# Attention in a one-core transformer kernel: values as the weights of the last product, probabilities scaled before they are turned, scores two steps ahead

## The chip, the core and the metric

The kernel runs on one core of one Trainium2 chip. The metric is the time on the device in microseconds (us), as the median of several executions. A core has TensorE (PE in the profile; its weight loads are PEld), VectorE (DVE), ScalarE (ACT), GpSimd (POOL) and SyncE (SP), which issues DMAs. Each has its own list of instructions, in a fixed order, and they wait for each other by semaphores. Matrix products go from the on-chip memory SBUF to the accumulator memory PSUM, which has eight banks of 128 partitions by 512 floats. GpSimd does not work on PSUM in this kernel.

## What is computed

The reference is a two-layer model on 1024 tokens of width 1024, in float32: a hybrid mixer and a feed-forward part, then a sparse attention mixer (16 heads of 64, two key groups) and a feed-forward part. The change lies in the attention, whose three branches are weighted with gates and summed:

```python
def attend_block(args):
    ...
    p_c = masked_softmax(s_c, (dist_c >= 0)[None, :, None, None, :])        # 63 compressed keys
    o_c = jnp.einsum('bqgjn,bngd->bqgjd', p_c, v_cmp)
    imp = jnp.einsum('bqgjn,nm->bqgm', p_c, cover)
    ...
    _, top = lax.top_k(imp, top_k)                                          # 6 blocks of 64 keys
    ...
    p_s = masked_softmax(s_s, (dist_s >= 0)[:, :, :, None], axis=(-2, -1))
    o_s = jnp.einsum('bqgjkl,bqgkld->bqgjd', p_s, v_g.astype(f32))
    ...
    p_w = masked_softmax(s_w, valid_w[None, :, None, None, :])              # window of 512
    o_w = jnp.einsum('bqgjs,bsgd->bqgjd', p_w, v_blk.astype(f32))
    o = g_blk[:, :, 0, :, :, None] * o_c + g_blk[:, :, 1, :, :, None] * o_s + g_blk[:, :, 2, :, :, None] * o_w
    return o.astype(h.dtype)
...
return o @ w_out
```

## The kernel before

The attention is a list `steps` of 144 steps. A step is (branch, first head, tile of 128 queries). Branch 2 is the compressed one: eight heads in one step, 63 keys each, 16 steps. Branch 1 is the window: two heads, one to five tiles of 128 keys, 64 steps. Branch 0 is the selected one: two heads, one to eight tiles of keys, 64 steps. Steps 0 to 79 mix compressed and window steps; mostly a compressed step is followed by two window steps of five tiles and one small one. In steps 80 to 143 the selected branch runs in couples: a query tile with many key tiles, then one with few, always nine tiles together (8 and 1, 7 and 2, 6 and 3, 5 and 4); each kind of couple comes eight times.

What one window or selected step does:
- TensorE, `scores(p)` (L1625; L1615 for the compressed branch): query by key products of two heads, 64 rows each, into PSUM banks 0 to 3.
- VectorE, `bias_step` (L1244): adds the bias, takes the minimum of the row, and writes the scores to SBUF (`SR`, four buffers, so two steps). `cmp_front` (L1161 to L1167) does this for the compressed branch, and GpSimd multiplies by the slopes (L558).
- ScalarE, `exp_step` (L792; L787): the exponential, with its sum in `STAT`.
- TensorE, `turn(p)` (L1642): turns (transposes) the probabilities, four tiles of 128x128 to a PSUM bank, in banks 4 and 5 by turns.
- ScalarE, `evacuate` (L804): copies each such group to SBUF (`PTR`).
- TensorE, `values(p)` (L1670; L1664): the turned probabilities are the weights (128x128), the values move (64 columns), the result lies with queries on partitions. It is issued inside `turn(p + 1)`, in as many parts as that step has groups, or in one piece at the end where it has one or two.
- VectorE, `out_step`: reciprocal of the sum (L1256), times the gate (L1257), and then two instructions (L1267) that scale each head's result and add it to `OACC`. For the compressed branch, `cmp_back` (L1174 to L1180) sums, takes the reciprocal, multiplies the gate and sums up the importance over the heads; `cmp_out` (L1196) scales.

The orders are written out by hand. TensorE: `scores(p+1)`, `turn(p)` with `values(p-1)` in it. VectorE: `bias_step(p+1)`, `cmp_back(p)`, `out_step(p-1)`, and at some steps `importance` and `select` (L1219 to L1224), which choose the blocks. ScalarE: `evacuate(p)`, `exp_step(p+1)`. GpSimd does the 16 slope products, and then adds the block bias of each couple (L568). Behind the last step TensorE turns all of `OACC` (L1688), ScalarE copies it to `YH` (L813), VectorE makes the low part `YL` (L1287), and the output product starts (L1312), whose weights GpSimd splits in a high and a low part (L403, L406); the first two of these splits stand ahead of the attention.

## Time and profile before

| | us |
|---|---|
| median of 3 runs | 3447.17 (3446.32 to 3450.53) |
| span of the profiled execution | 3455.9 |
| TensorE matmuls busy | 3161.6 (91%) |
| VectorE busy | 1405.7 (41%) |
| GpSimd busy | 1248.5 (36%) |
| ScalarE busy | 938.8 (27%) |
| attention, first to last step | about 1908 to 2581 of the span |

The profiled execution is 8.7 us longer than the median of the runs. A row of the page's list of groups gives line, engine, operation, output and inputs with their shapes, the count, the busy time and mean ns of one, and behind the last bar the idle time of the engine ahead of it and what ended that. A row of the timeline gives the start, the length in us (of several merged instructions: until the last one ends), the engine, line and operation. A float32 matmul has two records. PEclk is TensorE's granted clock as a share of full speed.

### The profile page before, as it was taken

The page shows a single profiled execution, that of the slowest core. Times are in us where ns is not written, and L with a number is a line of the kernel's source. Part 1 is how long each engine was busy: PE and PEld are TensorE (multiplying, and loading weights), DVE is VectorE, ACT ScalarE, POOL GpSimd, SP SyncE. Part 2 cuts the span into 40 slices and gives each one's busy share as a digit, 9 for nine tenths or more (in the row PEclk, how much of TensorE's full clock was granted, in tenths as well). Part 3 has the DMA queues.
Part 4 walks back from the last instruction along what each step waited for, and adds up shares of the span by engine and source line. Part 5 has one row for each costly group of instructions (what it writes and reads, how often), then busy time and mean ns, then how long its engine had stood idle before and what let it go on. Part 6 is the DMA issues. An engine that isn't in the chain of part 4 may idle for free. (4 is left out here: it accounts for less than half of the span.)

```text
span 3455.9 us, 41720 instructions
## 1 busy us (share of the span) xinstructions
PE 3161.6 (91%) x16629; PEld 2612.9 (76%) x16629; DVE 1405.7 (41%) x2167; ACT 938.8 (27%) x1447; POOL 1248.5 (36%) x638
## 2 busy tenths in 40 slices
PE   5967889887899999999897899999999899999998
PEld 4747887765778888888685787778878688888887
DVE  3675445353333133133301676655552332232334
ACT  3332223222133011021100454446661231010121
POOL 4325323465454444444642100000004544444442
PEclk8988999998899999999998897879999899999999
DMA  3100001110111111111114000000001111111111
GB/s 132 43 25 1 1 1 31 43 55 25 43 37 48 49 49 46 52 49 44 38 49 122 9 1 1 1 1 1 1 1 37 37 48 46 47 47 50 49 46 70
DMA packets 211543, 127.46 MB, mean 37 GB/s; under 512 B 8904, under 2 KB 208077, under 8 KB 211149
## 3 DMA queue, kind: packets, MB, share of 16 engines
q1 hardware_dynamic: 209600, 125.25, 12.3%
q8 instruction: 97, 1.59, 0.2%
q10 hardware_dynamic: 1805, 0.28, 0.0%
q14 instruction: 41, 0.34, 0.0%
HBM read 112.94 MB, written 8.39 MB: 35 GB/s over the span
## 5 line engine op out<-in xcount | busy, mean ns | idle before, releaser
L403 POOL TENSOR_TENSOR WH<-WR,ONES 128x1024 fp32r<-128x1024 f32 (+1 forms) x194 | 459.8, 2370 | 1355.1 <-PE PS L1312 1280.6
L1312 PE MATMUL PS<-YH,WH 128*128 128x512 f32 x2336 | 738.5, 398 | 63.5 <-POOL YL L428 34.9
L1312 PE MATMUL PS<-YL,WH 128*128 128x512 f32 x2336 | 726.6, 393 | 0.0
L1312 PE MATMUL PS<-YH,WL 128*128 128x512 f32 x2336 | 725.0, 392 | 0.0
L1312 PEld LDWEIGHTS PS<-YH,WH 128*128 128x128 f32 x2336 | 440.8, 190 | 178.5 <-issue 53.9
L1312 PEld LDWEIGHTS PS<-YL,WH 128*128 128x128 f32 x2336 | 444.0, 190 | 93.9
L1312 PEld LDWEIGHTS PS<-YH,WL 128*128 128x128 f32 x2336 | 442.5, 189 | 93.4
L406 POOL TENSOR_TENSOR WL<-WR,WH 128x1024 fp32r<-128x1024 f32 (+1 forms) x194 | 481.1, 2480 | 15.2
L1100 DVE SCALAR_TENSOR_TENSOR X<-PS,PTF,X 128x1023 f32<-128x1023 f32 (+1 forms) x176 | 225.6, 1282 | 573.4 <-ACT X L752 560.7
L752 ACT ACTIVATE X<-PS,PTF 128x1024 f32<-128x1024 f32 x88 | 106.2, 1207 | 840.5 <-PE PS L1312 840.3
L1670 PE MATMUL PS<-X,Z 128*128 128x64 f32 x2112 | 287.4, 287 | 0.0
L1670 PEld LDWEIGHTS PS<-X,Z 128*128 128x128 f32 x2112 | 282.2, 210 | 0.0
L804 ACT ACTIVATE Z<-PS 128x512 f32<-128x512 f32 (+2 forms) x336 | 175.8, 544 | 229.1 <-PE PS L1642 228.3
L1312 PE MATMUL PS<-MH,WH 128*128 128x512 f32 x704 | 217.3, 390 | 0.0
L1312 PE MATMUL PS<-MH,WL 128*128 128x512 f32 x704 | 216.8, 389 | 0.0
L1312 PE MATMUL PS<-ML,WH 128*128 128x512 f32 x704 | 216.7, 389 | 0.0
L1642 PE MATMUL PS<-IDENT,X 128*128 128x128 f32 (+1 forms) x1184 | 201.6, 300 | 8.1 <-ACT X L787 4.7
L1642 PEld LDWEIGHTS PS<-IDENT,X 128*128 128x128 f32 (+1 forms) x1184 | 142.0, 155 | 68.1 <-issue 56.7
L792 ACT ACTIVATE X<-X,STAT 128x640 f32<-128x640 f32 (+7 forms) x256 | 185.1, 728 | 28.6 <-DVE STAT L1244 28.6
L1625 PE MATMUL PS<-X 64*128 64x512 f32 (+3 forms) x768 | 167.0, 542 | 22.6 <-DVE STAT L1244 21.9
L1312 PEld LDWEIGHTS PS<-MH,WH 128*128 128x128 f32 x704 | 131.8, 188 | 28.9 <-DVE ML L1109 1.6
L1312 PEld LDWEIGHTS PS<-ML,WH 128*128 128x128 f32 x704 | 132.1, 188 | 27.5
(302 smaller groups left out, 3264.2 us busy)
## 6 DMA issues: line engine op xcount, KB each, us to landing
WR<-in_ffn_w_up_dram SPq DMA_DIRECT2D x88, 512.0 KB, 3.8
WR<-in_hy_w_in_dram SPq DMA_DIRECT2D x28, 512.0 KB, 3.8
WR<-in_ffn_w_down_dram SPq DMA_DIRECT2D x32, 448.0 KB, 3.6
WR<-in_ffn_w_down_dram SPq DMA_DIRECT2D x16, 512.0 KB, 3.7
WR<-in_nsa_w_in_dram SPq DMA_DIRECT2D x14, 512.0 KB, 3.7
Z<-in_x_dram SPq DMA_DIRECT2D x8, 512.0 KB, 7.5
xt_scratch<-H SPq DMA_DIRECT2D x1, 4096.0 KB, 12.1
H<-xt_scratch SPq DMA_DIRECT2D x1, 4096.0 KB, 12.3
```

Of the source, the lines that this page charges most:

```text
L403: pool.tensor_tensor(WH[:, slot, 0:k, :], WR[:, slot, 0:k, :], ONES[:, :].unsqueeze(1).broadcast_to([P, k, P]), ALU.mult).then_inc(w_hi, 1)
L406: pool.tensor_tensor(WL[:, slot, 0:k, :], WR[:, slot, 0:k, :], WH[:, slot, 0:k, :].bitcast(f32), ALU.subtract).then_inc(w_split, 1)
L752: act.activation(X[:, 16 + s, :], gemm_ps(s), ACT.Identity, scale=PTF[:, bass.ds(j + tap, 1)], bias=PTF[:, bass.ds(j + (C_FBIAS + l * 2 * ...
L792: act.activation(SR[n % 4][:, 0:w], SR[n % 4][:, 0:w], ACT.Exp, scale=-1.0, bias=STAT[:, 0, n % 8:n % 8 + 1], accum_out=STAT[:, 1, n % 8:n ...
L804: act.activation(PTR[p % 2][0:rows, i * 512:i * 512 + w], PS[0:rows, 4 + g % 2, 0:w], ACT.Copy).then_inc(pt_sb, 1)
L1100: dve.scalar_tensor_tensor(out=X[:, 16 + s, d:], in0=gemm_ps(s)[:, 0:SEQ - d], scalar=PTF[:, bass.ds(j + tap, 1)], in1=X[:, 16 + s, d:], o ...
L1312: ins = pe.matmul(PS[:, 2 * slot + a, :], w[:, slot, i, :], y[:, i, a * HALF:(a + 1) * HALF], start=(i == 0 and w is WH and y is hi), stop ...
L1625: ins = pe.matmul(gemm_ps(i)[:, a:e], X[part, h // 2, chunk(qt)], X[part, kt, first * P + a:first * P + e], start=True, stop=True)
L1642: ins = pe.transpose(PS[0:rows, 4 + g % 2, (k - 4 * i) * P:(k - 4 * i + 1) * P], src, IDENT[:, :])
L1670: ins = pe.matmul(PS[:, 6 + p % 2, i * DH:i * DH + DH], PTR[p % 2][:, k * P:(k + 1) * P], X[:, (VS, VW)[b], (first + t) * P + g * DH:(firs ...
```

## The change

- `values` swaps its operands: the values (64 columns) are the weights and the turned probabilities move (128 columns). Head i of the two writes partitions 64i to 64i+63 of the PSUM bank, so the result has head dimensions on partitions and queries along the free axis. The loop runs over key tiles outside and heads inside. `turn` lays the two heads' tiles alternately.
- Scaling by reciprocal and gate moves ahead of the turn: `norm_step` on VectorE takes the reciprocal only, and GpSimd's new `scale_step` multiplies the probabilities of each head in place with reciprocal and gate (for the compressed branch one product with the scale that `cmp_back` made, which waits for all of `cmp_back`). `turn(p)` waits for `scaled` in place of `p_ready`.
- `out_step` is one addition of 128x128 (or a copy) from PSUM; `cmp_out` is a copy.
- TensorE's order is `scores(p+2)`, `turn(p)`; VectorE's `bias_step(p+2)`, `norm_step(p+1)`, `out_step(p-2)`; ScalarE's `exp_step(p+1)`, `evacuate(p)`. `SR` has six buffers (three steps); the two new ones lie where `WL` lies.
- GpSimd adds the block bias of a couple three steps ahead of it. The first two splits for the output product move behind the last turn, since `WL` is taken until then.
- Behind the last step the turning of `OACC` is gone; ScalarE and VectorE read `OACC` itself.

TensorE, the turn of a five-tile window step with the values of a five-tile step ahead of it; before:

```order
2683 L1642 MATMUL PS<-IDENT,X 128x128 [waits att_p_ready,att_pt_sb]
2684 L1642 MATMUL PS<-IDENT,X 128x128 x3
2685 L1670 MATMUL PS<-X,Z 128x64 [waits att_pt_sb]
2686 L1670 MATMUL PS<-X,Z 128x64 x2
2687 L1642 MATMUL PS<-IDENT,X 128x128 [waits att_pt_sb]
2688 L1642 MATMUL PS<-IDENT,X 128x128 [waits att_p_ready]
2689 L1642 MATMUL PS<-IDENT,X 128x128 x2
2690 L1670 MATMUL PS<-X,Z 128x64 x3
2691 L1642 MATMUL PS<-IDENT,X 128x128 [waits att_pt_sb]
2692 L1642 MATMUL PS<-IDENT,X 128x128
2693 L1670 MATMUL PS<-X,Z 128x64 x4
```

The same place in the changed kernel (L1671 turns, L1699 multiplies by the values):

```order
2683 L1671 MATMUL PS<-IDENT,SRX 128x128 [waits att_scaled,att_pt_sb]
2684 L1671 MATMUL PS<-IDENT,SRX 128x128 [waits att_scaled]
2685 L1671 MATMUL PS<-IDENT,SRX 128x128 x2
2686 L1699 MATMUL PS<-Z,X 64x128 [waits att_pt_sb]
2687 L1699 MATMUL PS<-Z,X 64x128
2688 L1671 MATMUL PS<-IDENT,SRX 128x128 [waits att_pt_sb]
2689 L1671 MATMUL PS<-IDENT,SRX 128x128 x3
2690 L1699 MATMUL PS<-Z,X 64x128 x4
2691 L1671 MATMUL PS<-IDENT,SRX 128x128 [waits att_pt_sb]
2692 L1671 MATMUL PS<-IDENT,SRX 128x128
2693 L1699 MATMUL PS<-Z,X 64x128 x4
```

As many matmuls as before; each of the values now writes 64 partitions and moves 128 columns, and both waits for the probabilities stand at the front.

GpSimd around a compressed step of the changed kernel (L560 multiplies the slopes, L568 scales a compressed step, L576 a window step; before, only the slope products stood here):

```order
395 L560 TENSOR_TENSOR SRX<-SRX,SLOPE 128x504 [waits nsa_c_sub]
396 L576 TENSOR_SCALAR X<-X,STAT,SM 128x128 [waits att_r_ready]
397 L576 TENSOR_SCALAR X<-X,STAT,SM 128x128
398 L568 TENSOR_TENSOR SRX<-SRX,CST 128x504 [waits nsa_imp_c]
399 L576 TENSOR_SCALAR X<-X,STAT,SM 128x640 [waits att_r_ready]
400 L576 TENSOR_SCALAR X<-X,STAT,SM 128x640
401 L576 TENSOR_SCALAR X<-X,STAT,SM 128x640 [waits att_r_ready]
402 L576 TENSOR_SCALAR X<-X,STAT,SM 128x640
```

The scaling of the compressed step waits for `imp_c`, the last instruction of `cmp_back`, and the two larger steps are scaled behind it.

The core of the diff:

```diff
@@ turn
-                        j, t = divmod(k, tiles)
-                        if t == 0:
-                            pe.wait_ge(p_ready, 2 * p + j + 1)
+                        if k < 2:
+                            pe.wait_ge(scaled, 2 * p + (2 if b == 2 else k + 1))
@@ values
-                    for k in mine:
-                        i, t = divmod(k, tiles)
-                        ins = pe.matmul(PS[:, 6 + p % 2, i * DH:i * DH + DH], PTR[p % 2][:, k * P:(k + 1) * P],
-                                        X[:, (VS, VW)[b], (first + t) * P + g * DH:(first + t) * P + g * DH + DH],
-                                        start=(t == 0), stop=(t == tiles - 1))
+                    for t in mine:
+                        for i in range(2):
+                            ins = pe.matmul(PS[head_part(i), 6 + p % 2, 0:P],
+                                            X[:, (VS, VW)[b], (first + t) * P + g * DH:(first + t) * P + g * DH + DH],
+                                            PTR[p % 2][:, (2 * t + i) * P:(2 * t + i + 1) * P], start=(t == 0), stop=(t == tiles - 1))
@@ gpsimd
+            def scale_step(p):
+
+                b, h, qt = steps[p]
+                if b == 2:
+                    pool.wait_ge(imp_c, cmp_no[p] + 1)
+                    pool.tensor_tensor(scores_of(p), scores_of(p), CST[:, cmp_no[p] % 2, 2, :].unsqueeze(2).broadcast_to([P, JH, NC]),
+                                       ALU.mult).then_inc(scaled, 2)
+                    return
+                w = keys_of(qt, b)[1] * P
+                pool.wait_ge(r_ready, p + 1 - cmp_no[p + 1])
+                for i in range(2):
+                    n = 2 * p + i
+                    gate = (1 + b) * H16 + h + i
+                    pool.tensor_scalar(SR[n % 6][:, 0:w], SR[n % 6][:, 0:w], STAT[:, 2, n % 8:n % 8 + 1], GATE[:, qt, gate:gate + 1],
+                                       ALU.mult, ALU.mult).then_inc(scaled, 1)
...
+            slope_step(0)
+            for p in range(len(steps)):
+                if p + 1 < len(steps):
+                    slope_step(p + 1)
+                c, before = divmod(p + 3 - SELECTED, PER_COUPLE)
+                if before == 0 and 0 <= c < len(couples):
+                    couple_bias(c)
+                scale_step(p)
+            pool.wait_ge(tr_done, pair_groups[len(steps)])
+            splits(U_NOUT, 2)
@@ vector
+            def norm_step(p):
...
+                dve.reciprocal(STAT[:, 2, at:at + 2], STAT[:, 1, at:at + 2]).then_inc(r_ready, 1)
...
             for p in range(len(steps)):
+                if p + 2 < len(steps):
+                    bias_step(p + 2)
                 if p + 1 < len(steps):
-                    bias_step(p + 1)
-                if steps[p][0] == 2:
-                    cmp_back(p)
-                if p >= 1:
-                    out_step(p - 1)
+                    norm_step(p + 1)
+                if p >= 2:
+                    out_step(p - 2)
@@ scalar
             for p in range(len(steps)):
-                evacuate(p)
                 if p + 1 < len(steps):
                     exp_step(p + 1)
+                evacuate(p)
+            act.wait_ge(o_used, len(steps))
             for m in range(MT):
-                act.wait_ge(ot_ready, m + 1)
-                act.activation(YH[:, m, :], gemm_ps(m % 2), ACT.Copy).then_inc(ot_hi, 1)
+                act.activation(YH[:, m, :], OACC[:, m, :], ACT.Copy).then_inc(ot_hi, 1)
@@ tensor
             scores(0)
+            scores(1)
             for p in range(len(steps)):
-                if p + 1 < len(steps):
-                    scores(p + 1)
+                if p + 2 < len(steps):
+                    scores(p + 2)
                 turn(p)
             values(len(steps) - 1, 0, 1)
-            pe.wait_ge(o_used, 2 * len(steps))
-            for m in range(MT):
-...
```

## Rows read from the trace of the kernel before

**Rows 1.** Groups by line and shape, 1908 to 2597 us: the values matmul.

```profile
L1670 PE MATMUL PS<-X,Z 128*128 128x64 f32 x2112 | 287.4, 287 | 0.0
```

**Rows 2.** Windows: stretch, its length, busy us of each engine (count), granted clock.

```profile
1908.00:2230.00 322.00, 300.36 (x2111) 251.66 (x2112) 221.26 (x610) 157.50 (x365) 22.21 (x25) 0.84 0.00 1
2230.00:2305.00 75.00, 67.70 (x360) 51.42 (x357) 44.65 (x143) 33.60 (x86) 4.47 (x4) 0.73 0.00 1
2305.00:2581.00 276.00, 273.50 (x2123) 224.30 (x2121) 140.92 (x518) 182.02 (x416) 13.55 (x12) 1.00 0.01 1
```

**Rows 3.** Timeline of one couple of eight and one tiles, selected branch.

```profile
2309.42 1.99 PE L1625 MATMUL PS<-X 64*128 64x512 f32 x8
...
2311.61 3.68 PE L1670 MATMUL PS<-X,Z 128*128 128x64 f32 x32
...
2312.80 1.15 ACT L792 ACTIVATE X<-X,STAT 128x1024 f32<-128x1024 f32 x1 [0.55 <-DVE STAT L1244]
...
2315.22 0.49 PE L1625 MATMUL PS<-X 64*128 64x128 f32 x4
...
2315.65 1.09 PE L1642 MATMUL PS<-IDENT,X 128*128 128x128 f32 x8
...
2317.74 1.09 ACT L804 ACTIVATE Z<-PS 128x512 f32<-128x512 f32 x2 [0.26 <-PE PS L1642]
...
2318.30 1.99 PE L1625 MATMUL PS<-X 64*128 64x512 f32 x8
```

**Rows 4.** Timeline of TensorE in the earlier mixer: matmuls with 64-column weights.

```profile
725.21 0.38 PE L1510 MATMUL PS<-IDENT,X 128*128 128x128 f32 x2
725.78 0.45 PE L1525 MATMUL PS<-H 128*64 128x128 f32 x4 [0.19 <-issue]
...
727.33 0.44 PE L1526 MATMUL PS<-H 128*64 128x128 f32 x4
727.70 1.13 PE L1531 MATMUL PS<-H 128*128 128x256 f32 x4
```

**Rows 5.** Groups by line and shape, GpSimd over the whole span.

```profile
L403 POOL TENSOR_TENSOR WH<-WR,ONES 128x1024 fp32r<-128x1024 f32 x162 | 391.7, 2418 | 1184.7 <-PE PS L1312 1110.1 <-DMA WR<-in_nsa_w_out_dram 55.0 <-DMA WR<-in_hy_w_in_dram 19.6
...
L568 POOL TENSOR_TENSOR Z<-Z,SM 128x1024 f32<-128x1024 f32 x2 | 3.8, 1900 | 0.0
...
L552 POOL TENSOR_SCALAR_AFFINE_SELECT Z<-Z 128x1024 f32<-128x1024 f32 x1 | 1.1, 1087 | 0.1
```

**Rows 6.** Line L558: ns min/median/max, first and last start of its 16 instructions.

```profile
L558 POOL TENSOR_TENSOR X<-X,SLOPE x16: 1027/1028/1031, 1934.3 to 2208.6; 128x504 f32<-128x504 f32 x16
```

**Rows 7.** Timeline around compressed steps.

```profile
2149.82 0.81 DVE L1244 CUSTOM_DVE_ANT_0 X<-PS,X 128x640 f32<-128x640 f32 x1
...
2151.31 0.67 DVE L1174 TENSOR_REDUCE CST<-X 128x8 f32<-128x504 f32 x1
...
2153.38 1.06 DVE L1180 TENSOR_REDUCE Z<-Z 128x63 f32<-128x504 f32 x1
...
2161.84 0.68 DVE L1161 TENSOR_TENSOR X<-PS,Z 128x504 f32<-128x504 f32 x1 [0.57 <-issue]
...
2164.24 1.03 POOL L558 TENSOR_TENSOR X<-X,SLOPE 128x504 f32<-128x504 f32 x1 [14.86 <-DVE X L1167]
2164.27 1.01 DVE L1257 TENSOR_TENSOR STAT<-STAT,SM 128x2 f32<-128x2 f32 x1
```

**Rows 8.** Timeline of the end of the attention.

```profile
2580.70 0.47 DVE L1267 SCALAR_TENSOR_TENSOR Z<-PS,STAT,Z 128x64 f32<-128x64 f32 x2 [1.05 <-PE PS L1670]
...
2593.81 2.36 DVE L1287 TENSOR_TENSOR YL<-PS,YH 128x1024 fp32r<-128x1024 f32 x2 [1.11 <-ACT YH L813]
2596.22 0.50 PEld L1312 LDWEIGHTS PS<-YH,WH 128*128 128x128 f32 x2 [2.61 <-DVE YL L1287]
2596.22 1.22 PE L1312 MATMUL PS<-YH,WH 128*128 128x512 f32 x2 [2.38 <-DVE YL L1287]
```

**Rows 9.** Windows of TensorE alone: length, busy us (count), granted clock.

```profile
2244.00:2246.00 2.00, 0.70 (x7) 1.00 0.00 0
2246.00:2248.00 2.00, 0.95 (x4) 0.95 0.00 0
2248.00:2250.00 2.00, 2.00 (x10) 0.50 0.00 0
```

101 lines of the change are left out of this document (49 added, 52 removed).

## Prediction, made before the changed kernel was run

> **What bounds the kernel now.** I read the shares of busy time first: TensorE is busy for 91% of the span. The change touches only the attention, 1908 to 2596 us, so I then read windows over it [rows 2]. In the selected branch (2305 to 2581) TensorE is busy for 273.5 of 276 us at full clock: it is the bound, 8.6 us per couple for 32 couples. In the compressed and window steps (1908 to 2230) it is busy for 300 of 322 us, but at a granted clock of 0.84, and VectorE is busy for 221 us; here waits on VectorE and a clock that falls behind them cost as much as TensorE's work. A cycle of one compressed and three window steps takes 15.9 us where it runs undisturbed (GpSimd's slope product comes 14.86 + 1.03 us after the one ahead of it [rows 7]) and 18.3 us on average ((2208.6 - 1934.3) / 15 [rows 6]). Last I read the timeline of one couple [rows 3]: scores, the values of the step ahead and the turn follow each other with hardly a gap.
>
> **Values as weights.** Before, 32 records (8 tiles, two heads) go from 2311.61 to 2315.22 [rows 3], 0.11 us each, 0.44 us per tile for both heads. The new form stands in the trace already: the earlier mixer multiplies with 64-column weights and writes the two halves of the partitions alternately. There seven groups of four records go by between 725.78 and 727.33 [rows 4], 0.055 us each, although each moves 128 columns, twice as many as L1670. The two halves run side by side. So a tile costs 0.22 us, half. The selected branch has 288 of the 528 tiles (2112 records / 4 [rows 1]), and the saving there is 288 x 0.22 = 63 us.
>
> **The switch between forms.** The new form is entered from a turn and left to a turn or to scores. In the trace the first 64-column matmul starts 0.46 us after the last turn's start (725.78 against 725.21 + 0.11), where 0.11 is the pace: 0.35 lost. On the way out 0.20 goes by (727.70 against 727.33 + 3 x 0.055), 0.1 lost [rows 4]. The 0.35 may hold some of the five semaphore waits in front of that matmul, so a switch into it costs between 0.1 (as the way out) and 0.35, and a piece of values 0.2 to 0.45 in all. I take 0.3, between the ends, since two waits stand there now. By the code, values come in 106 pieces in the selected branch, 3.3 per couple: +32 us. This speaks against the change where `turn` cuts values into parts of one tile. The Trainium skill, TensorEngine Tiling (Array Packing), section Tiling Modes, says that a change of tiling mode drains TensorE; the trace agrees, since the next weight load waits for the matmul ahead. The same page, Performance Considerations, recommends just this swap for 64 columns, at up to twice the speed; by that alone, with no drain, the selected branch would save 63 us less the wait of the ring below.
>
> **A chain of waits in the selected branch.** ScalarE takes `exp_step(p+1)` only after `evacuate(p-1)`. For a couple of 8 and 1 tiles the ring is: turn of the wide step to its last copy, 3.2 us (2315.65 to 2317.74 + 1.09); two exponentials, 2 x 1.15 + 0.1 = 2.4 [rows 3]; reciprocal and semaphores, 0.3; two scalings on GpSimd; 0.1 to the next wide turn. GpSimd's new instruction has one tensor input and is not in the trace. The nearest rows at 1024 elements are 1.09 us for a select in place with one input, 1.90 for a product of two tensors, and 2.42 where it also writes fp32r [rows 5]. I take 1.05, nearest in form to the first. The ring is then 6.0 + 2.1 = 8.1 us. TensorE's own work in this couple is 8.9 - 9 x 0.22 + 2 x 0.3 = 7.5, so these eight couples wait 0.6 us each, +5. For narrower ones every term of the ring shrinks, and TensorE stays the bound. The Trainium skill, GPSIMD Engine Reference, section 3.1, gives 1.03 cycles per element at 1.2 GHz for one input, an estimate of 0.88 us for 1024; with it the ring would be 7.8 us. No row shows this instruction itself.
>
> Selected branch together: -63 + 32 + 5 = -26 us.
>
> **The compressed steps.** Before, TensorE turned the probabilities right after the exponential, and `cmp_back` ran beside it. Now the turn waits for `cmp_back` and GpSimd's product, and VectorE reaches `cmp_back(q)` only behind `bias_step(q+1)`. From the end of `scores(q+1)`: bias of five tiles 1.5 us (2149.82 to 2151.31), `cmp_back` 3.1 (2151.31 to 2153.38 + 1.06), product 1.03, as L558 [rows 7], semaphores 0.3, together 5.9. TensorE has in that time a small turn with the values of a five-tile step (0.3 + 1.1 + 0.3) and scores of five tiles (about 5/8 of the 1.9 us between 2309.42 and the next turn [rows 3], and an overhead, 1.4), 3.1 us. It stands still for 2.8 us per cycle. Against that its work shrinks: 11 tiles x 0.22 = 2.4, compressed values 16 records x 0.055 = 0.9, and about 8 pieces x 0.3 = 2.4 come on top (125 pieces in these 16 cycles). 15.9 - 0.9 - 0.6 (an idle time that goes) + 2.8 = 17.2 us. So the undisturbed cycle gets 1.2 longer, 15 x 1.2 = +18 us. The clock costs 18.3 - 15.9 = 2.4 us per cycle now; it fell to 0.5 here after 4 us in which TensorE was busy for 1.65 [rows 9]; standing still becomes more frequent, but less work is left to run slowly. I leave it at 2.4.
>
> VectorE's instructions with two SBUF inputs wait while GpSimd works: L1257 takes 1.01 us beside L558 [rows 7]. GpSimd will work about a third of the time, and some of `cmp_back` and `select` can be hit; I have no more than this row for it, up to 1 us per cycle, 0 to +15, and take 0, since GpSimd has by the order little to do in these moments.
>
> **The other steps.** Steps 64 to 79 (2230 to 2305) have 54 tiles, -12, and 16 pieces, +5: -7 us. At step 77 GpSimd waits for the last `select` and adds the first couple's bias (about 2.3 us, 1.90 for the wide half [rows 5]) ahead of the scaling that the turn waits for: bias, select (six instructions, five of them over 512 elements at the 0.7 us of L1161 [rows 7], 3.6), 2.3 and two scalings make 9 us of standing still where TensorE had some 2 before: +7. Together 0.
>
> **The end.** From the last addition to the first output product 15.5 us go by (2580.70 to 2596.22 [rows 8]). The turns go; what is left is one copy (about the 1.15 of an exponential of that size [rows 3]) and eight `YL` of 1.2 (2.36 for two), 11 us. But `YL` now has two SBUF inputs, and GpSimd's four split instructions of some 2.4 [rows 5] run beside it; they hold VectorE up by 0 to 6 us. I take 4.5: 0 in all, -4 to +2. The splits themselves stay hidden behind `YL`; TensorE waits for VectorE before and after.
>
> Sum: -26 + 18 + 0 + 0 = -8 us, made on the profiled execution of 3455.9 us; the median lies 8.7 lower and I take the difference from it: 3439 us.
>
> **Rivals.**
> 1. *The compressed steps don't add.* For it: TensorE runs at 0.84 of its clock there [rows 2], and if it is up for more of the time, 300 busy us at 0.84 have up to 48 us to give. Against it: the 2.8 us of standing still. With 0 for the cycles, and pieces at 0.2 (-11): 3447 - 37 = 3410.
> 2. *The clock decides, slower.* Each cycle's 2.8 us is about as long as the idle time ahead of the fall to half [rows 9]. If every one does, some 5 us of work run slowly and cost 2 more per cycle: 3439 + 30 = 3469. It decides from about 0.5 us per cycle on.
> 3. *GpSimd is slow.* At 1.90 us for 1024 the ring is 9.8, 8.9, 8.1 and 7.6 us for the four kinds of couple, 8.6 on average, and the saving of 26 is gone. In the window steps two scalings of 640 (2 x 0.5 more) lie behind the compressed one: +15. 3439 + 26 + 15 = 3480.
> 4. *The halves don't run side by side here* (two heads' operands from one bank and buffer): values cost as before and the pieces come on top: 63 back in the selected branch, 12 in steps 64 to 79 and some 25 in the cycles, 3539. Rows 4 speak against it; 3 in 100.
>
> **Chances.** Forecast 0.40 (its own range 3425 to 3452), rival 1 0.27, rival 2 0.18, rival 3 0.12, rival 4 0.03. A measurement of this kernel can tell about 0.2%, 7 us. Faster: rival 1 and nearly 0.6 of the forecast, 0.50. Same: 0.16. Slower: 0.34. The range 3405 to 3476 leaves out rival 4, most of rival 3 and the far ends of the other two.
>
> **What would show it.** Values records at a pace of 0.055 us, with 0.1 to 0.35 us lost on the way into each piece; couples of 8 and 1 at 8.1 us that wait for GpSimd, the others near 7.7 with TensorE without gaps; TENSOR_SCALAR of 1024 near 1.05 us; compressed steps at which TensorE waits some 2.8 us for GpSimd, and `cmp_back` ahead of it. I am wrong if the turns wait in most couples, if the granted clock of the selected branch falls below 1.00, or if the cycles keep 18 us.

## The result, and the profile of the changed kernel

The changed kernel takes 3449.45 us (median of 20 runs, 3438.31 to 3452.08), the kernel before 3438.30 us in the 20 runs beside it (3428.19 to 3450.53). The ratio is 1.0029, 95% interval 1.0017 to 1.0040: **the change makes the kernel slower by 0.3%, some 10 us**. The forecast was 3439 us and faster. The time lies within the range of 3405 to 3476; the direction is the wrong one. The three runs of the kernel before from which the prediction started (3447.17) were from the upper part of its spread; these 20 runs gather near 3429, 3438 and 3448, and what sets which of them one gets stayed open. Of the kernels further down, one execution each of fill12, oldvalues and onepiece took 5.5 to 7.8 ms; the ratios leave it out, the medians hold it and are 0.3 to 1.4 us higher for it.

The first view is that of the windows: stretch, its length, busy time (count) of TensorE, its weight loads, VectorE, ScalarE and GpSimd, granted clock, DMA share and GB/s. They answer to [rows 2].

```profile
1908.00:2230.00 322.00, 267.13 (x1858) 179.79 (x1859) 176.93 (x467) 137.52 (x320) 102.45 (x123) 0.73 0.00 1
2230.00:2305.00 75.00, 62.34 (x530) 38.64 (x529) 47.51 (x143) 46.90 (x118) 30.63 (x38) 0.99 0.00 1
2305.00:2317.00 12.00, 3.19 (x18) 2.60 (x20) 5.11 (x12) 1.55 (x3) 5.04 (x6) 0.58 0.00 0
2317.00:2571.00 254.00, 245.60 (x2172) 158.44 (x2170) 112.61 (x388) 180.69 (x424) 122.42 (x145) 0.99 0.01 1
```

Up to 2230 TensorE is busy for 267 instead of 300 us and has got less far, 1858 records instead of 2111: its granted clock is 0.73 on average where it was 0.84. Behind 2305 it stands nearly still for 9 us, and the selected branch behind it is short. GpSimd, at 22 us of 322 before, now has 102.

The cycles are counted as in [rows 6], by the first and the last slope product of the 16 compressed steps, in the timeline of GpSimd:

```profile
1932.19 1.03 POOL L560 TENSOR_TENSOR X<-X,SLOPE 128x504 f32<-128x504 f32 x1 [3.01 <-DVE X L1197]
...
2239.17 1.03 POOL L560 TENSOR_TENSOR X<-X,SLOPE 128x504 f32<-128x504 f32 x1 [3.79 <-DVE X L1197]
```

307.0 us for 15 cycles, 20.5 each; [rows 6] gave 18.3. A second profile of the kernel before (below) gives 18.5. So the cycles lose 30 us, and that is the loss; the two stages behind them gain. By landmarks (last slope product; the first bias of the selected branch on GpSimd; the end of the last values; the first output product):

| us | before, second profile | change | change minus before |
|---|---|---|---|
| 15 cycles | 277.2 | 307.0 | +29.8 |
| last slope product to first bias | 80.0 | 71.3 | -8.7 |
| first bias to last values | 283.6 | 261.0 | -22.6 |
| last values to first output product | 15.6 | 16.2 | +0.6 |

From the first output product to the end of the program it is 859.8 us in the change and 856.7 in this profile of before (859.7 in its first one), so the two spans, 3447.4 and 3445.0, differ by 2.4 us.

One bias on GpSimd serves four couples of the same kind, eight steps. Such a group of four is called a set here; its time is the distance between its bias and the next on GpSimd. The recorded expectations say "couple" for it where they give 28 to 36 us.

The waits that the prediction worked out for a compressed step are in the trace nearly to the number. Here is one compressed step, all engines:

```profile
2151.86 0.82 DVE L1270 CUSTOM_DVE_ANT_0 X<-PS,X 128x640 f32<-128x640 f32 x1
...
2153.35 0.67 DVE L1204 TENSOR_REDUCE CST<-X 128x8 f32<-128x504 f32 x1
...
2155.42 1.05 DVE L1210 TENSOR_REDUCE Z<-Z 128x63 f32<-128x504 f32 x1
...
2156.63 1.03 POOL L568 TENSOR_TENSOR X<-X,CST 128x504 f32<-128x504 f32 x1 [6.93 <-DVE Z L1210]
...
2157.80 1.94 PE L1671 MATMUL PS<-IDENT,X 128*63 128x128 f32 x8 [2.96 <-POOL X L568]
```

From the bias of the five-tile step (2151.86) over `cmp_back` (2153.35 to 2155.42 + 1.05) and GpSimd's product L568 to the turn that waits for it (2157.80) it takes 5.9 us, as worked out, and TensorE stands still for 2.96 us; 2.8 was forecast. What comes behind it is this (windows again):

```profile
2150.00:2160.00 10.00, 6.40 (x50) 4.40 (x50) 8.14 (x21) 2.93 (x7) 2.69 (x3) 0.84 0.01 2
2160.00:2170.00 10.00, 10.00 (x58) 6.73 (x54) 2.30 (x9) 4.78 (x13) 1.80 (x3) 0.50 0.01 2
```

In the 10 us in which this pause lies TensorE is busy for 6.4, and in the next 10 its granted clock is 0.50, the lower of its two levels. Two microseconds at a time, TensorE alone, around the pause of another cycle:

```profile
2020.00:2022.00 2.00, 1.64 (x16) 1.00 0.00 0
2022.00:2024.00 2.00, 0.00 (x0) 0.93 0.00 0
2024.00:2026.00 2.00, 1.40 (x7) 0.50 0.00 0
```

The clock falls within the pause and stays at 0.50 up to 2040. Nine of the 16 compressed turns have a pause of 2.95 or 2.96 us and another four one of 2.26 to 3.46, and of the 28 windows of 10 us from 1950 to 2230 only 4 are at 0.98 or more; 10 are in the second profile of before.

The values and their switches (TensorE, the turn of six tiles with which the third set begins, and behind it the scores of three tiles):

```profile
2391.06 1.09 PE L1671 MATMUL PS<-IDENT,X 128*128 128x128 f32 x8
2392.09 0.44 PE L1699 MATMUL PS<-Z,X 128*64 128x128 f32 x4
2392.47 0.66 PE L1671 MATMUL PS<-IDENT,X 128*128 128x128 f32 x4
2393.05 0.44 PE L1699 MATMUL PS<-Z,X 128*64 128x128 f32 x4
2393.42 0.92 PE L1655 MATMUL PS<-X 64*128 64x384 f32 x4
```

A turn of four transposes starts at 2392.47, and the values behind it at 2393.05: 0.58 us for 4 x 0.11, so 0.14 on the way in. The four values records take until 2393.42, 0.37 for 4 x 0.055, so 0.15 on the way out. A piece costs 0.29 us (0.3 was taken), and the pace of 0.055 is that of [rows 4], where [rows 3] had 0.11.

A couple of 8 and 1 tiles, where the wide turn was to wait for GpSimd (it answers to [rows 3]):

```profile
2456.90 1.14 ACT L823 ACTIVATE X<-X,STAT 128x1024 f32<-128x1024 f32 x1
...
2458.16 0.17 DVE L1281 RECIPROCAL STAT<-STAT 128x2 f32<-128x2 f32 x1 [1.50 <-ACT X L823]
...
2458.43 2.37 POOL L576 TENSOR_SCALAR X<-X,STAT,SM 128x1024 f32<-128x1024 f32 x2 [3.09 <-DVE STAT L1281]
...
2460.15 0.33 PE L1671 MATMUL PS<-IDENT,X 128*128 128x128 f32 x1
...
2460.85 0.98 PE L1671 MATMUL PS<-IDENT,X 128*128 128x128 f32 x7 [0.38 <-POOL X L576]
...
2462.15 1.15 PE L1671 MATMUL PS<-IDENT,X 128*128 128x128 f32 x8 [0.31 <-ACT Z L835]
```

Second exponential 2456.90, reciprocal 2458.16, two scalings of 1024 columns in 2.37 us from 2458.43 on, the wide turn's first transpose when the scores ahead of it are done (2460.15), and then 0.38 us of waiting for the second scaling and 0.31 for ScalarE's copies. The ring is there, with small pauses.

GpSimd's new instruction by width (groups, 2317 to 2572 us; mean ns of one behind the comma):

```profile
L576 POOL TENSOR_SCALAR X<-X,STAT,SM 128x1024 f32<-128x1024 f32 x10 | 11.9, 1195 | 12.2 <-DVE STAT L1281 12.2
...
L576 POOL TENSOR_SCALAR X<-X,STAT,SM 128x128 f32<-128x128 f32 x10 | 4.4, 448 | 9.4 <-DVE STAT L1281 9.4
```

1.20 us for 1024 columns, 0.45 for 128: some 0.34 us for the instruction and 0.83 ns per column. The Trainium skill, GPSIMD Engine Reference, section 3.1, has 1.03 cycles per element, an estimate of 0.86 ns per column: the slope agrees with the trace, and what the estimate of 0.88 us in the prediction left out is the 0.34.

Step 77, where the selected branch begins, and the end of the attention (which answers to [rows 8]):

```profile
2310.19 0.18 DVE L1251 TENSOR_SCALAR SM<-Z 128x32 f32<-128x32 f32 x1
2310.45 2.25 POOL L588 TENSOR_TENSOR Z<-Z,SM 128x128 f32<-128x128 f32 x2 [8.40 <-DVE SM L1251]
2312.69 1.52 POOL L576 TENSOR_SCALAR SRX<-SRX,STAT,SM 128x512 f32<-128x512 f32 x2
...
2313.60 0.45 PE L1671 MATMUL PS<-IDENT,SRX 128*128 128x128 f32 x1 [8.65 <-POOL SRX L576]
```
```profile
2571.49 0.29 DVE L1295 TENSOR_TENSOR Z<-Z,PS 128x128 f32<-128x128 f32 x1 [0.58 <-PE PS L1699]
2571.81 7.68 ACT L844 ACTIVATE YH<-Z 128x1024 fp32r<-128x1024 f32 x8 [1.74 <-DVE Z L1295]
...
2572.90 14.65 DVE L1317 TENSOR_TENSOR YL<-Z,YH 128x1024 fp32r<-128x1024 f32 x8 [1.12 <-ACT YH L844]
2574.16 3.35 POOL L406 TENSOR_TENSOR WH<-WR,ONES 128x1024 fp32r<-128x1024 f32 x1
...
2587.61 1.22 PE L1342 MATMUL PS<-YH,WH 128*128 128x512 f32 x2 [16.16 <-DVE YL L1317]
```

TensorE stands still for 8.65 us behind the last select (to 2310.37), the first bias (2.25) and the first scaling. At the end the eight `YL` take 14.65 us, 1.83 each where [rows 8] had 1.18. The first three run beside GpSimd's splits and take 2.40, 3.37 and 3.36 us, the other five 1.21, and a split takes 3.35 us where [rows 5] had 2.42.

### The profile page after: what moved, and what is told of

Read it like the earlier page. It is cut to its first block and busy times, and to the rows that moved or that the text cites. A ratio compares the mean times of both kernels' runs of the same rounds, so it can differ in the third digit from the quotient of the medians.

```text
span 3447.4 us, 41440 instructions
## 1 busy us (share of the span) xinstructions
PE 3092.4 (90%) x16565; PEld 2460.8 (71%) x16565; DVE 1347.5 (39%) x1910; ACT 933.5 (27%) x1447; POOL 1469.3 (43%) x910
## 5 line engine op out<-in xcount | busy, mean ns | idle before, releaser
L576 POOL TENSOR_SCALAR X<-X,STAT,SM 128x640 f32<-128x640 f32 (+7 forms) x170 | 133.9, 797 | 157.2 <-DVE STAT L1281 157.2
L1671 PE MATMUL PS<-IDENT,X 128*128 128x128 f32 (+1 forms) x784 | 150.3, 323 | 41.6 <-POOL X L568 27.6
L1699 PE MATMUL PS<-Z,X 128*64 128x128 f32 x2112 | 175.7, 301 | 0.0
L1655 PE MATMUL PS<-X 64*128 64x512 f32 (+3 forms) x768 | 158.2, 519 | 16.7 <-DVE STAT L1270 15.7
L1671 PEld LDWEIGHTS PS<-IDENT,X 128*128 128x128 f32 (+1 forms) x784 | 97.7, 159 | 98.6 <-issue 68.2
L1342 PEld LDWEIGHTS PS<-MH,WL 128*128 128x128 f32 x704 | 132.2, 188 | 27.5
```

The source lines that it names most:

```text
L576: pool.tensor_scalar(SR[n % 6][:, 0:w], SR[n % 6][:, 0:w], STAT[:, 2, n % 8:n % 8 + 1], GATE[:, qt, gate:gate + 1], ALU.mult, ALU.mult).th ...
L1342: ins = pe.matmul(PS[:, 2 * slot + a, :], w[:, slot, i, :], y[:, i, a * HALF:(a + 1) * HALF], start=(i == 0 and w is WH and y is hi), stop ...
L1655: ins = pe.matmul(gemm_ps(i)[:, a:e], X[part, h // 2, chunk(qt)], X[part, kt, first * P + a:first * P + e], start=True, stop=True)
L1671: ins = pe.transpose(PS[0:rows, 4 + g % 2, (k - 4 * i) * P:(k - 4 * i + 1) * P], src, IDENT[:, :])
L1699: ins = pe.matmul(PS[head_part(i), 6 + p % 2, 0:P], X[:, (VS, VW)[b], (first + t) * P + g * DH:(first + t) * P + g * DH + DH], PTR[p % 2][ ...
```

## The experiments

All ratios are against the kernel before, run on the same chip beside the kernel (its medians were 3439.6 in the first four runs, 3443.1 in the second four and 3442.4 in the last two), with 95% intervals; the change stands at 1.0029. Where kernels of different groups are compared below by their medians, the 3.5 us between these medians of before are in the difference.

### The kernel before, once more

No edit.

> The kernel before, unchanged, for a second profile: the one shown ran in 3455.9 us, above the median of 3438 over 20 runs, so differences between its trace and that of the change are not those between the medians. Theory A (the clock varies from run to run in the attention's first part): a run of about 3430 to 3440 us with the same work and waits, but a higher granted clock than 0.84 between 1908 and 2230 us or than 0.73 between 2230 and 2305 us. Theory B (the difference lies elsewhere): the same clock there, and the 10 to 20 us somewhere else.

3447.5 us (one execution), span 3445.0. Theory A's time was not met: this run is no fast one either. It shows that two executions differ where the clock does: 80.0 instead of 89.6 us from the last slope product to the first bias, while the cycles add up to nearly the same (277.2 and 274.3). Its row over the cycles and the longest pause in it:

```profile
1950.00:2230.00 280.00, 265.70 (x1842) 222.79 (x1842) 194.51 (x536) 137.90 (x320) 14.41 (x14) 0.83 0.00 1
```
```profile
2110.86 2.50 PE L1625 MATMUL PS<-X 64*128 64x512 f32 x8 [3.59 <-DVE STAT L1244]
```

Behind a `select` the scores wait 3.59 us for VectorE, and from there to 2160 the 10-us windows show 0.50 to 0.69. So the kernel before loses to the clock as well, in fewer places: [rows 9] was one of them.

### Keeping TensorE busy in the pauses: the change (fill12) and the kernel before (before_fill)

```diff
 turn, behind the wait for the PSUM bank that it writes (fill12)
+                    for _ in range(12 if b == 2 and i == 0 else 0):
+                        pe.matmul(PS[:, 4 + g % 2, 0:P], IDENT[:, :], IDENT[:, :], start=True, stop=True)
```

> The change, with 12 products of the identity with itself (128 columns, fp32, about 0.22 us each at full clock, 2.6 us together) on TensorE ahead of each of the 16 compressed turns, in the PSUM bank that the turn writes next. They compute nothing that is used. In the change's trace TensorE stands still for 2.96 us ahead of nearly every one of these turns and the granted clock then falls to 0.50 for some microseconds. Theory A (the fall of the clock is the price, the waiting alone nearly nothing more than 2.96 us a cycle): the clock stays near 1.00 between 1950 and 2230 us, the cycles take 16.7 to 17.5 us instead of 20.5 and the kernel is 30 to 55 us faster than the change, 3395 to 3420 us. Theory B (the chain of VectorE and GpSimd sets the cycle, whatever the clock): 12 more products change nothing or cost up to 16 x 1 us, 3445 to 3465 us.

3402.9 us, ratio 0.9898 (0.9870 to 0.9927). Theory A holds, to its numbers: 46 us gained over the change by adding 192 products that nobody reads.

```diff
 the kernel before, ahead of the scores that wait for VectorE behind a select (before_fill)
+            late = {first_select[g] + 3 * k + 1 + 3 for g in range(NG) for k in range(TT // 2)}
...
+                if q in late:
+                    if g >= 2:
+                        pe.wait_ge(pt_sb, g - 1)
+                    for _ in range(8):
+                        pe.matmul(PS[:, 4 + g % 2, 0:P], IDENT[:, :], IDENT[:, :], start=True, stop=True)
```

> The kernel before, with 8 products of the identity with itself (1.8 us at full clock) on TensorE ahead of the 16 scores that wait for VectorE behind a select, where TensorE stands still for 1.9 to 3.6 us in the trace and the granted clock falls to 0.50 behind most of them. Nothing uses them. Theory A (the clock makes the kernel before slow here too, and makes its runs spread from 3428 to 3457 us): the clock stays near 1.00, cycles of compressed and window steps go from 18.4 to about 16.5 us on average, 15 to 35 us are gained and the spread shrinks; then against this kernel, not against the one before, must the change be held where the clock is kept up. Theory B (the clock falls for another reason than these pauses): 0 to 10 us slower.

3421.2 us, ratio 0.9937 (0.9921 to 0.9954): 22 us, within theory A's 15 to 35, and its 6 runs lie within 11 us (3414 to 3425) where the 23 of the kernel before spread over 22. The rows over 1950 to 2230, first of fill12, then of before_fill:

```profile
1950.00:2230.00 280.00, 263.16 (x2324) 187.64 (x2321) 185.04 (x499) 149.15 (x356) 107.02 (x128) 0.96 0.01 1
```
```profile
1950.00:2230.00 280.00, 268.13 (x2034) 224.66 (x2033) 207.17 (x579) 147.41 (x345) 14.42 (x14) 0.92 0.00 1
```

0.96 and 0.92, where the change had:

```profile
1950.00:2230.00 280.00, 235.50 (x1598) 158.06 (x1597) 153.37 (x401) 118.63 (x273) 85.61 (x101) 0.72 0.00 1
```

The length of each of the 15 cycles, by the starts of the slope products:

```
before (2nd)  4.3 16.3 17.9 17.6 16.4 17.8 16.3 16.4 23.5 25.6 29.6 21.0 20.8 17.6 16.3   277.2
before_fill   4.3 16.3 17.8 17.6 16.4 17.8 16.3 18.0 22.4 20.1 22.8 15.9 19.7 19.4 16.3   261.0
change        4.1 16.2 16.3 21.5 24.2 24.0 24.0 21.7 20.9 16.9 24.9 24.0 23.5 24.1 20.7   307.0
fill12        4.1 17.7 18.0 16.8 16.8 16.9 16.8 17.0 20.4 17.2 24.5 19.8 16.8 16.8 16.8   256.7
sig           4.1 14.6 15.3 16.8 16.8 16.8 16.8 16.8 20.4 19.6 25.5 19.8 19.4 18.9 16.8   258.5
```

This is the case in five lines. With its pause filled and its clock full, a cycle of the change takes 16.8 us, half a microsecond more than the 16.3 of before. With the pauses open it takes 24 us, again and again: the pause of 2.96 us brings the clock down, at half clock the work takes longer, and the clock comes back some 4 us before the next pause. The kernel before loses most at the selects (cycles 9 to 13). Filled, the two are nearly even over the cycles (256.7 and 261.0), and the kernels stand at 3402.9 and 3421.2: **with the pauses filled in both, the change is 18 us faster by the medians** and 13 by the two ratios, whose intervals leave 2 to 25 (the runs themselves don't overlap: 3400 to 3404 and 3414 to 3425). Between the first bias and the last values, where the clock is full in both but for fill12's first microseconds, it gains 20.1 us (260.9 against 281.0). The comparison isn't quite even elsewhere: before_fill fills the pauses at the selects and fill12 those of the compressed turns, and each keeps some stretches at half clock.

The fillers have a price too. In the second and third cycle the change's pauses ahead of compressed turns are 2.48 and 1.64 us or none, and the fill of 2.9 us (4.3 at half clock) makes these cycles 17.7 and 18.0 us long, where the change has 16.2 and 16.3 and sig (next) 14.6 and 15.3.

### A shorter pause (sig)

```diff
-                link(dve.tensor_tensor(CPN, cs, rs.unsqueeze(2).broadcast_to([P, JH, NC]), ALU.mult))
+                dve.tensor_tensor(CPN, cs, rs.unsqueeze(2).broadcast_to([P, JH, NC]), ALU.mult).then_inc(cpn_ready, 1)
+                dve.wait_ge(cpn_ready, cmp_no[p] + 1)
...
-                    pool.wait_ge(imp_c, cmp_no[p] + 1)
+                    pool.wait_ge(cpn_ready, cmp_no[p] + 1)
```

> The change, with GpSimd's scaling of a compressed step released one VectorE instruction earlier: after the product that writes the copy for the importance, not after the reduction behind it (1.06 us). Theory A (the chain bias, the back half of the compressed step, scaling is what TensorE waits for): its standing still ahead of compressed turns falls from 2.96 to about 1.9 us, 16 us in all, and if the shorter pause no longer lets the clock fall, up to 45 us: 3400 to 3435 us. Theory B (something else, such as ScalarE's copies or buffers, is right behind): under 5 us.

3403.1 us, ratio 0.9898 (0.9873 to 0.9924), by releasing GpSimd's product in each compressed step one VectorE instruction earlier. Theory A's time is met, but its first part, 16 us for the shorter wait itself, hardly shows. The pause did get shorter:

```profile
2007.15 1.06 PE L1672 MATMUL PS<-IDENT,X 128*63 128x128 f32 x8 [1.60 <-POOL X L568]
```

1.60 us instead of 2.96, at a granted clock of 1.00 in all 10-us windows from 1960 to 2080. But its undisturbed cycles are 16.8 us, like those of fill12, which keeps the long chain: of the 1.06 us that came off the compressed turn nothing is left in the cycle, because the turns behind it wait 0.38 and 0.46 us for the scalings of the next step. So in these cycles the shorter chain by itself gains nothing; nearly all of the 46 us is the clock.

### The swap alone (oldvalues, oldvalues_fill)

```diff
-                            ins = pe.matmul(PS[head_part(i), 6 + p % 2, 0:P], X[:, (VS, VW)[b], ...],
-                                            PTR[p % 2][:, (2 * t + i) * P:(2 * t + i + 1) * P], ...)
+                        ins = pe.matmul(PS[:, 6 + p % 2, i * DH:i * DH + DH], PTR[p % 2][:, (2 * t + i) * P:(2 * t + i + 1) * P],
+                                        X[:, (VS, VW)[b], ...], ...)
```

> The change, with the operands of the values products in the old places: probabilities as weights, 64 columns of values moved (its output is laid out wrongly, the work and the order are the change's). It prices the swap alone. Theory A (values 0.44 against 0.22 us per tile, some 0.1 to 0.3 us lost per piece): the selected branch takes 30 to 45 us longer than in the change. In the compressed steps TensorE has some 3 us more work a cycle in front of the same chain; the total is 3480 to 3500 us where the clock there stays as in the change, and 3455 to 3475 us where the added work keeps the clock up. Theory B (the swap buys nothing, the gain of the selected branch came from the order two steps ahead): within 10 us of the change.

3538.7 us, ratio 1.0303 (1.0268 to 1.0338), above both of theory A's ranges. Its runs spread from 3521 to 3556, and the profiled one is the fastest of them. There the selected part takes 298.0 us, 37 more than in the change, as expected; the cycles take 22.7 us each at a granted clock of 0.68, which was not. TensorE has more work there and a lower clock still.

> The run with the values' operands in their old places (3539 us; its output is laid out wrongly), with 12 products of the identity ahead of each compressed turn. It parts the swap's price from the clock's. Theory A (of its 89 us over the change, 37 in the selected branch are the swap and the rest is a clock that falls even more often): the clock stays up, the cycles take 18 to 19.5 us instead of 22.7, 3470 to 3490 us. Theory B (the cycle of 22.7 us is work and waits, not clock): 3530 us or more.

3475.2 us, ratio 1.0102 (1.0086 to 1.0117), within theory A's 3470 to 3490: cycles of 19.1 us, selected part 298.1. So with the compressed turns' pauses filled the swap is worth 72 us by the medians (3475.2 against 3402.9) and 66 by the spans of the two profiles; 37 of these are in the selected part and 30 in the cycles. And the other half of the change, scaling ahead of the turn and scores two steps ahead, costs 54 us by the medians (3475.2 against before_fill's 3421.2) and 45 by the spans: 25 in the cycles, 6 in steps 64 to 79, 17 in the selected part with step 77, less 1 at the end and 2.5 ahead of the cycles. Some of that is still the clock, since this kernel's pauses at the selects aren't filled and before_fill's are.

### GpSimd's place in the selected branch (narrow)

```diff
-                w = keys_of(qt, b)[1] * P
+                w = P if b == 0 else keys_of(qt, b)[1] * P
                 pool.wait_ge(r_ready, p + 1 - cmp_no[p + 1])
```

> The change, with GpSimd's scaling in the selected branch cut to the first 128 columns of each row (the other columns stay unscaled, so the output is wrong), about 0.45 us an instruction instead of up to 1.20. It prices GpSimd's place in the selected branch. Theory A (the ring of copies, exponentials, scaling and the next wide turn sets the couples of 8 and 1 tiles, TensorE the others): the two couples whose periods are 35 and 33.8 us in the change (8 and 1) get 3 to 6 us shorter each, the couples at 29.1 to 30.5 us by under 0.5 us; 6 to 12 us in all. Theory B (GpSimd is hidden everywhere): under 2 us. Theory C (GpSimd's scaling is late in every couple): 15 us or more.

3443.6 us, ratio 1.0002 (0.9989 to 1.0016), 6 us less from the first bias to the last values (255.0 against 261.0). The fifth set (8 and 1 tiles), in the change and here:

```profile
2435.04 2.26 POOL L588 TENSOR_TENSOR Z<-Z,SM 128x128 f32<-128x128 f32 x2
...
2468.82 2.26 POOL L588 TENSOR_TENSOR Z<-Z,SM 128x256 f32<-128x256 f32 x2
```
```profile
2432.01 2.26 POOL L588 TENSOR_TENSOR Z<-Z,SM 128x128 f32<-128x128 f32 x2
...
2463.91 2.26 POOL L588 TENSOR_TENSOR Z<-Z,SM 128x256 f32<-128x256 f32 x2
```

33.8 us against 31.9, so 0.5 us for each of the four couples; the other kinds get 0.5 us shorter a set or not at all (30.5 to 30.0, 29.1 to 28.6, 29.5 to 29.7). It is theory A in kind, and its total of 6 to 12 is met at the low end; but it had 3 to 6 us for each set of 8 and 1, and 2.1 and 1.9 were measured. The ring binds in the couples of 8 and 1, and it is worth 4 us.

### The first bias behind step 77's scaling (latebias)

```diff
-                if before == 0 and 0 <= c < len(couples):
+                if before == 0 and 0 < c < len(couples):
                     couple_bias(c)
                 scale_step(p)
+                if before == 0 and c == 0:
+                    couple_bias(c)
```

> The change, with the first couple's bias on GpSimd behind the scaling of step 77 instead of ahead of it (the other couples' places stay). In the change's trace TensorE stands still for 8.65 us at the turn of step 77, behind the last select, this bias (2.25 us) and the scaling, and the granted clock is 0.60 and 0.84 in the 20 us behind it. Theory A (the order on GpSimd is the cause): the turns of steps 77 and 78 go ahead during the select, the pause of 8.65 us is cut or moved to step 79, 3 to 6 us shorter, and with the clock 5 to 10 us are gained over the change in this stage. Theory B (the select itself and the order on VectorE hold the branch's start, whoever goes first on GpSimd): the pause only moves, under 3 us.

3439.8 us, ratio 0.9989 (0.9976 to 1.0001). From the first bias to the last values it takes 253.6 instead of 261.0 us: 7.4 us gained in this place, theory A. Four of its 12 runs are near 3430 and eight near 3440, and the profiled one is of the four; its cycles took 297 us and not 307. The pause is cut from 8.65 us:

```profile
2303.61 0.30 PE L1673 MATMUL PS<-IDENT,X 128*128 128x128 f32 x1 [4.80 <-POOL X L576]
```

### All of it together (combined, onepiece)

```diff
 combined: sig, latebias, 7 products ahead of each compressed turn, 6 ahead of the scores behind a select, and
+            for _ in range(60):
+                pe.matmul(PS[:, 4, 0:P], IDENT[:, :], IDENT[:, :], start=True, stop=True)
 behind the last values
```

> The change with four things: the scaling of compressed steps released behind the product (as in the run that did this alone), the first couple's bias behind step 77's scaling, and products of the identity with itself in TensorE's pauses: 7 ahead of each compressed turn, 6 ahead of the scores that wait behind a select, 60 (13 us) behind the last values, where TensorE stands still for 16.2 us and then runs at half clock for some 6 us. Theory A (the clock is what is lost, and the pauses are free to be filled): 3403 us less about 5 for the end, less 5 to 10 for the selects, less 5 to 10 for step 77: 3380 to 3390 us, granted clock at 0.95 or more in every 10 us of the attention. Theory B (the earlier release alone has got what there is): 3398 to 3405 us.

3393.9 us, ratio 0.9859 (0.9842 to 0.9875): between the theories, 9 us better than sig or fill12 alone. 5.6 us are gained in the selected part (255.3 against fill12's 260.9) and 2 in the stage ahead of it. The cycles are not better (261.5 us): theory A wanted a clock of 0.95 or more in every 10 us, and there are stretches at 0.63 to 0.68. The end:

```profile
2521.39 13.66 PE L1729 MATMUL PS<-IDENT 128*128 128x128 f32 x120
2537.67 0.74 PE L1345 MATMUL PS<-YH,WH 128*128 128x512 f32 x2 [2.62 <-DVE YL L1320]
```

The wait at the end is as long as before (16.2 us, the 60 products fill 13.7 of it), and the ten microseconds behind it now have a clock of 1.00 where the change has 0.69. That is worth little: from the first output product to the end it takes 858.5 us here, 859.5 in fill12 and 858.0 in sig.

```diff
-                    if p >= 1 and groups <= 2:
-                        if i == groups - 1:
-                            values(p - 1, 0, 1)
-                    elif p >= 1:
-                        values(p - 1, i, groups)
+                    if p >= 1 and i == min(1, groups - 1):
+                        values(p - 1, 0, 1)
```

> The run with four things together (3394 us), with the values of a step in one piece behind the second group of the next turn, instead of a piece behind each of its three or four groups. In the selected branch that takes away 40 of 106 pieces (1, 2 and 2 for each pair of steps of 7 and 2, 6 and 3, 5 and 4 tiles; none for 8 and 1). Theory A (each piece costs some 0.3 us of TensorE, 0.15 on the way in and 0.15 on the way out, as the change's trace has it, and TensorE is the bound there): 12 us less, 3382 us; the couples at 30.5, 29.1 and 29.5 us get 1.2, 2.4 and 2.4 us shorter, those of 8 and 1 stay. Theory B (the pieces cover ScalarE's copies, which the third and fourth group wait for; in one piece that cover is lost): 0 to 5 us slower.

**3374.8 us, ratio 0.9806 (0.9791 to 0.9821), the fastest of all, 1.9% faster than the kernel before.** 19 us were gained where theory A had 12, and in another place. In the selected part it is only 4.8 (250.5 us), and not where it was expected: the sets of 7 and 2 and of 6 and 3 tiles stay (30.7 against 30.5, 29.0 against 29.1), that of 5 and 4 gets 1.5 shorter (28.1 against 29.5) and that of 8 and 1, which loses no piece, 0.7 (33.1 against 33.8).

```profile
2320.60 1.27 PE L1676 MATMUL PS<-IDENT,X 128*128 128x128 f32 x8
2321.80 0.66 PE L1701 MATMUL PS<-Z,X 128*64 128x128 f32 x8
2322.39 0.66 PE L1676 MATMUL PS<-IDENT,X 128*128 128x128 f32 x4
2322.98 0.92 PE L1658 MATMUL PS<-X 64*128 64x384 f32 x4
```

This is the passage of which the change's rows stand above, with one piece of eight records where it had two of four. From the turn to the scores it takes 2.38 us here (2320.60 to 2322.98) and 2.36 there (2391.06 to 2393.42): a piece fewer, and nothing gained. One reason is in the last two rows: from the turn of four to the scores it takes 0.59 us for 4 x 0.11, so leaving a turn for the scores costs the same 0.15 as leaving it for values; a piece that stood between turn and scores saves one switch and not two. At 0.15 for each of 40 pieces it would be 6 us, and 4.8 were measured, but the sets don't bear this sum out one by one. The first eight transposes also take 1.20 us here and 1.03 there. Over the selected part the waits of TensorE and its weight loads for ScalarE's copies (theory B) stay at 17 us; but TensorE's matmuls now wait 13.6 us for GpSimd's scalings, 19 times, where it was 9.3 us and 12 times in combined, so GpSimd takes back a part of what the pieces give. In the cycles 17 us were gained (244.5 against 261.5): where the clock is full in both, a cycle falls from 16.8 to 15.8, and in the fourth and fifth it was low in combined (22.0 and 18.8 us, here 15.8 each).

## Why the prediction was wrong, point by point

The forecast was -8 us and the medians differ by +11. The step that failed is the clock in the compressed steps, left at 2.4 us a cycle where the pauses of the change add another 2.4. That the time still came within 10 us of the forecast is luck: the clock term was some 34 us too low, and the cycle's own length some 22 us too high.

- **What bounds the kernel**: right. TensorE is busy for 245.6 of 254 us in the selected branch; the compressed steps are bound by waits and the clock.
- **Values at half the price**: right; 0.055 us a record. oldvalues shows that the selected part is 37 us longer without it, where -63 + 32 = -31 was worked out, or -26 with the ring.
- **The switch, 0.3 a piece**: right in the trace for a piece between two turns (0.14 and 0.15), too much for one between a turn and scores, which adds one switch and not two; the passage of onepiece shows it. The way out in [rows 4] is 0.15 as well, with the records' own pace of 0.055 taken off (727.70 - 727.33 - 4 x 0.055); the prediction took off 0.11 and had 0.1.
- **The ring, +5**: right. narrow puts it at 0.5 us a couple (0.6 forecast). GpSimd's instruction takes 1.20 instead of the 1.05 taken, and a set of 8 and 1 takes 33.8 us, 8.45 a couple, instead of 8.1.
- **Selected branch, -26**: right. Measured per set, in the second profile of before and in the change: 8 and 1 tiles 35.5 to 33.8, 7 and 2 34.3 to 30.5, 6 and 3 33.8 to 29.1, 5 and 4 33.5 to 29.5; -14.2 for the four kinds, -28 for the eight sets.
- **The pause in the compressed steps**: right, 5.9 us of chain and 2.96 of standing still (2.8 forecast).
- **The cycle's own length, 15.9 to 17.2, +18**: mis-sized. An undisturbed cycle went from 16.3 to 16.8; 15.9 was the shortest of before and not the usual one [rows 7]. Over all fifteen, fill12 takes 256.7 us and before_fill 261.0, so with the pauses filled the term is -4. Part of that is clock: before_fill is at 0.92 and fill12 at 0.96.
- **The clock, "I leave it at 2.4" a cycle**: this is the step that failed. By fill12 the clock takes 50 us from the change's cycles (307.0 against 256.7), 3.6 from each of the 14 full ones; by before_fill 16 from before's (277.2 against 261.0), 1.2 each. Neither fill brings the clock to 1.00 throughout, so the true figures are larger. By these two the change adds 2.4 a cycle, +34 us. The prediction had the fact in hand, in its rival 2 (+2 a cycle): a pause about as long as the idle time ahead of the fall in [rows 9], in every cycle. It then held that less work is left to run slowly, and gave that rival 0.18. The excess of 2.4 a cycle that it left in was itself a mean that had one short cycle of 4.3 us among its 15.
- **Rival 1** (3410 us: the cycles add nothing) is near what the change does with its pauses filled: fill12 has 3403.
- **VectorE beside GpSimd, taken 0**: small but not 0. The two instructions of each `select` that read two SBUF inputs right behind its first one, first in the change, then before:

```profile
L1247 DVE TENSOR_TENSOR Z<-Z 128x512 f32<-128x512 f32 x8 | 8.7, 1092 | 0.3
L1248 DVE TENSOR_TENSOR Z<-Z 128x512 f32<-128x512 f32 x8 | 8.0, 1004 | 0.3
```
```profile
L1220 DVE TENSOR_TENSOR Z<-Z 128x512 f32<-128x512 f32 x8 | 5.5, 692 | 0.3
L1221 DVE TENSOR_TENSOR Z<-Z 128x512 f32<-128x512 f32 x8 | 5.5, 692 | 0.3
```

  5.7 us in all 16 of them. The Trainium skill, Trainium Architecture — The Big Picture, section What this means for kernel authors, has the port that VectorE and GpSimd share as an exclusive lock and not as a split bandwidth. The rows agree as far as they go: instructions are longer where the engines meet, VectorE's here and both at the end, where a `YL` takes 1.21 us alone and up to 3.37 beside the splits. No run here tells a lock from shared bandwidth by a test of its own.
- **Steps 64 to 79, -7**: -8.7 by the second profile of before, but with before_fill (70.9 us) and fill12 (74.4) it is +3.5. The gain was the clock, which fell in before (80.0 and 89.6 us in its two profiles); before_fill has it at 1.00 here and fill12, which fills nothing in these steps, at 0.83 to 0.85 in two of the 10-us windows.
- **Step 77, +7**: right; TensorE stands still for 8.65 us where 9 was worked out. latebias gets 7.4 back with a pause of 4.80 left, so a part of the price is again the clock behind it.
- **The end, 0**: +0.6. `YL` is held up by 5.2 us (14.65 - 8 x 1.18), 4.5 taken.
- **The base**: the forecast was made against 3447.17. Against the 3438.3 of 20 runs the same working would have given 3430.

Put together, in us against the kernel before:

| | forecast | pauses filled (fill12 - before_fill) | as built (change - second profile of before) |
|---|---|---|---|
| cycles | +18 | -4.3 | +29.8 |
| steps 64 to 79 | -7 | +3.5 | -8.7 |
| selected branch with step 77 | -26 + 7 | -20.1 | -22.6 |
| end | 0 | +0.6 | +0.6 |
| sum | -8 | -20.3 | -0.9 |

The middle column is mostly the change's work and waits, and the kernels differ by 18.3 us in their medians (3402.9 and 3421.2). The last column is of two single executions, in which before's was slower than its median; by the medians the change is 11 us slower.

Open: which executions of the kernel before fall into the slower cycles (none of its profiled ones was near 3430), so how the 10 us between the medians split can't be read from a trace; and what sets the undisturbed cycle of 16.8 us, since a chain shorter by 1.06 us left it as it was, while values in one piece brought it to 15.8.

## What to carry to other kernels

Where TensorE's granted clock is below 1.00 in a stage, cost a new wait not by its length but by the work behind it that will run at half clock: here pauses of 2.96 us made cycles of 24 us out of cycles of 16.8. Before giving such a change up, try the two cheap cures: release the waiting instruction as early as its data allow, or give TensorE something to do in the pause; each turned +0.3% into -1.0% here. Fill no more than the pause: where it was shorter than the fill, cycles got 1.5 and 1.7 us longer. And work out a cycle's undisturbed length from several cycles, not from the shortest.

## What was not expected of the hardware

- A steady state of its own: seven cycles of 23.5 to 24.9 us, six with a pause of 2.95 or 2.96 us and one with 3.46, each with a fall to 0.50 and a return some 4 us before the next pause.
- The length of a pause alone doesn't tell whether the clock falls. In sig it was at 1.00 from 1960 to 2080 with pauses of 1.60 to 1.97 us and TensorE busy for 6.9 to 9.9 us of each ten; in the second profile of before it fell to 0.50 behind one of 1.90 (ending at 1945.60), ahead of which TensorE had been busy for 9.1 of 10 us.
- A high busy share is no sign of a high clock: oldvalues is busy for 259 of 280 us (1950 to 2230) at 0.68, sig for 232 of 280 at 0.92. At half clock the same work is busy for nearly twice as long: the compressed turn of eight takes 1.94 us in the change and 1.06 in sig.
- Products of a 128 x 128 identity that nobody reads cost next to nothing in a pause that is as long as they are: in the steady cycles fill12 takes 16.8 us, like sig.
